# Chunked scan of a hybrid decoder layer: B transposed as two row tiles, and the z transposes placed ahead of the first twelve gate products

## What is computed

```python
def step(state, inp):
    xc, ac, bc, cc = inp
    cs = jnp.cumsum(ac, axis=1)
    seg = cs[:, :, None] - cs[:, None, :]
    lmat = jnp.exp(jnp.where(causal, seg, -jnp.inf))
    cb = jnp.einsum("blgn,bsgn->blsg", cc, bc)
    y_diag = jnp.einsum("blsg,blsgj,bsgjp->blgjp", cb, lmat, xc)
    y_off = jnp.einsum("blgn,bgjpn,blgj->blgjp", cc, state, jnp.exp(cs))
    decay = jnp.exp(cs[:, -1:] - cs)
    new_state = (state * jnp.exp(cs[:, -1])[..., None, None]
                 + jnp.einsum("blgn,blgj,blgjp->bgjpn", bc, decay, xc))
    return new_state, y_diag + y_off
...
y = y + xs * d_skip
yg = y * silu(z)          # then a norm over each group, and norm_w
gates = sigmoid(merge)    # merge is the last part of the input projection
```

## Time and profile before

| | us |
|---|---|
| median of 3 runs | 2771.94 |
| lowest, highest | 2771.37, 2773.98 |
| the profiled execution | 2769.81 |
| its span | 2768.2 |
| PE busy in it | 2684.8 |
| DVE, POOL, ACT busy | 1531.2, 1487.4, 1175.7 |

### The profile page before, as it was taken

The page is one execution under the profiler, slowest core; times in us unless marked ns, Lnnn a source line. Parts: engine busy times, 40 slices in busy tenths (PEclk is TensorE's granted clock), DMA queues, the critical chain, the costliest instruction groups (busy, mean ns, idle before and its releaser), DMA issues. The chain is left out here.

```text
span 2768.2 us, 45651 instructions
## 1 busy us (share of the span) xinstructions
PE 2684.8 (97%) x17046; PEld 2203.3 (80%) x17046; DVE 1531.2 (55%) x2475; ACT 1175.7 (42%) x2207; POOL 1487.4 (54%) x1055
## 2 busy tenths in 40 slices
PE   6999999999999999999999899999899999999998
PEld 5888888888887788888888677777788877788787
DVE  6335322599452523786532565665788885843432
ACT  6232232233223532333232556566677854532332
POOL 7778767777786777777875455454000254232000
PEclk8999999999999999999999999999999999999999
DMA  3557433333224333332233555564777578954543
GB/s 127 141 172 212 141 107 122 97 114 110 62 76 154 135 124 98 114 108 84 76 94 113 185 187 182 163 197 163 205 218 198 149 234 266 310 170 152 190 137 113
DMA packets 469469, 415.30 MB, mean 150 GB/s; under 512 B 43328, under 2 KB 414272, under 8 KB 464192
## 3 DMA queue, kind: packets, MB, share of 16 engines
q1 hardware_dynamic: 467008, 404.81, 47.4%
q0 software_dynamic: 2304, 8.39, 0.8%
HBM read 282.60 MB, written 130.55 MB: 149 GB/s over the span
## 5 line engine op out<-in xcount | busy, mean ns | idle before, releaser
L547 PE MATMUL p_acc<-h_kept,w_hi 128*128 128x512 f32 x1216 | 476.0, 391 | 6.5 <-ACT work L603 3.1
L549 PE MATMUL p_acc<-h_kept,w_lo 128*128 128x512 f32 x1216 | 474.6, 390 | 0.0
L548 PE MATMUL p_acc<-h_kept,w_hi 128*128 128x512 f32 x1216 | 474.6, 390 | 0.0
L428 POOL TENSOR_TENSOR w_lo<-p_sums,w_hi 128x512 fp32r<-128x512 f32 x300 | 387.5, 1306 | 149.3 <-ACT w_hi L644 149.3
L644 ACT ACTIVATE w_hi<-p_sums 128x512 fp32r<-128x512 f32 x300 | 189.7, 633 | 505.3 <-PE p_acc L549 482.9
L272 DVE TENSOR_TENSOR p_stage<-p_acc,work 128x512 f32<-128x512 f32 x172 | 138.2, 806 | 275.3 <-PE p_acc L549 267.9
L547 PEld LDWEIGHTS p_acc<-h_kept,w_hi 128*128 128x128 f32 x1216 | 228.9, 188 | 56.4 <-ACT work L603 3.3
L549 PEld LDWEIGHTS p_acc<-h_kept,w_lo 128*128 128x128 f32 x1216 | 229.1, 188 | 47.7
L548 PEld LDWEIGHTS p_acc<-h_kept,w_hi 128*128 128x128 f32 x1216 | 229.0, 188 | 46.9
L547 PE MATMUL p_acc<-p_ops,w_hi 128*128 128x512 f32 x608 | 238.2, 392 | 5.7 <-DVE p_ops L743 5.7
L548 PE MATMUL p_acc<-p_ops,w_hi 128*128 128x512 f32 x608 | 237.5, 391 | 0.0
(11 more groups left out here) (335 smaller groups left out, 6069.9 us busy)
## 6 DMA issues: line engine op xcount, KB each, us to landing
raw<-w_in SPq DMA_DIRECT2D x100, 512.0 KB, 4.7
work<-s_gates SPq DMA_DIRECT2D x48, 512.0 KB, 7.1
p_rawb<-w_in SPq DMA_DIRECT2D x38, 512.0 KB, 3.7
keep<-w_in SPq DMA_DIRECT2D x38, 512.0 KB, 4.8
s_xbc<-p_stage SPq DMA_DIRECT2D x32, 512.0 KB, 2.6
work<-s_xbc SPq DMA_DIRECT2D x16, 1024.0 KB, 6.3
att_all<-s_att SPq DMA_DIRECT2D x24, 528.0 KB, 5.2
s_gates<-p_stage SPq DMA_DIRECT2D x24, 512.0 KB, 6.0
```

The costliest lines, as they stand in the source:

```text
L428: tt(w_lo[:, k], weight(u, k), w_hi[:, k], ALU.subtract).then_inc(w_made, 1)
L547: pe.matmul(bank, hi, ops[k][:, 0, c], start=c == 0, stop=False)
L548: pe.matmul(bank, hi, ops[k][:, 1, c], start=False, stop=False)
L549: last = pe.matmul(bank, lo, ops[k][:, 0, c], start=False, stop=c == 3)
```

## The change

B is transposed by the helper `transpose_by_rows`: eight 64-row instructions in place of four of 128 rows. The upper rows go into the first half of the first bank of `ps_m`, the lower ones into half of a new bank `ps_b`. ACT copies B out in two instructions of 128x256 in place of one of 128x512. The wait for `out_taken` before it becomes an instruction of its own (`wait_alone`). The z transposes, with their two waits, move ahead of `gates(0)`, so that `gates(0)` and `gates(1)` stand in a row.

```diff
+        ps_b = s.ps("s_psb", [P, BANK])
...
+        b_banks = [ap[:, :GROUPS * P // 2].rearrange("p (g q) -> p g q", q=P // 2) for ap in (ps_m, ps_b)]
...
-                        pe.wait_ge(out_taken, 2 * c + 1)
+                        wait_alone(pe, out_taken, 2 * c + 1, turn_released)
                         for g in range(GROUPS):
-                            last = pe.transpose(ps_m[:, g * P:(g + 1) * P], b_t[:, g], ident[:])
+                            last = transpose_by_rows(pe, [b_bank[:, g] for b_bank in b_banks], b_t[:, g], ident)
                         last.then_inc(b_transposed, 1)
                         pe.wait_ge(out_taken, 2 * c + 2)
                         for g in range(GROUPS):
                             last = pe.matmul(ps_m[:, BANK + g * P:BANK + (g + 1) * P], b_t[:, g], c_t[:, g],
                                              start=True, stop=True)
                         last.then_inc(cb_ready, 1)
-                        gates(0)
                         pe.wait_ge(z_loaded[k], 16 * i + 16)
                         wait_alone(pe, x_tok_ready, c + 1, turn_released)
                         for b in range(KC):
                             last = transpose_by_rows(pe, [z_bank[:, b] for z_bank in in_banks(ps_x)], z_t[:, k, b], ident)
                         last.then_inc(z_transposed, 1)
+                        gates(0)
                         gates(1)
...
-                        act.activation(b_tok[:], ps_m[:, :BANK], ACT.Copy).then_inc(b_tok_ready, 1)
+                        for half in range(2):
+                            at = slice(half * P // 2, (half + 1) * P // 2)
+                            last = act.activation(b_tok[:].rearrange("p (g q) -> p g q", q=P)[:, :, at], b_banks[half], ACT.Copy)
+                        last.then_inc(b_tok_ready, 1)
```

## The result

The changed kernel takes 2779.25 us (median of 7 runs, 2775.37 to 2780.55); the kernel before took 2769.41 us beside it (7 runs, 2764.96 to 2773.98). The ratio is 1.0035, with a 95% interval of 1.0023 to 1.0047: slower by about 9.8 us. Its profiled execution has a span of 2776.2 us, 8.0 us more than before.

The account below looks back on a forecast made before the run. PE, busy 97% with in-order work, was taken as the bound; 7.9 - 0.6 + 4.1 = +11.4 us on 2771.9 gave 2783.3 us, with 2781 to 2786 by the bounds (73%) and 2776 to 2789 as the 8-in-10 range.

Parts of the forecast that it names:

- the two signs of a wrong forecast: z starting before the copy of x ends behind a load, or granted clock leaving 1.00 between 1560 and 1958.
- The exposed wait: Chunks 2 to 12, even: PE waits 1.48 us before z for ACT's copy of x; net 6 x 1.31 = +7.9 us.
- Joined products and odd chunks: Odd chunks and chunk 14: joining blocks saves 0.17 us, z waits 0.1; nine times, -0.6 us, bounds -1.2 and 0.
- Chunk 0: Scan's first chunk: moved products no longer fit before z, +2.4 us, plus 1.7 for the clock; +4.1 us.
- The low clock: Chunk 0, behind z: after some 4 us of waiting products may run at half speed; +1.7 us, bounds 0 and 2.5.
- B as row tiles: B before CB: a shorter B only leaves PE waiting for ACT's second copy of y; 0 us.
- The second copy on ACT: ACT's copy of B in two: 0.1 to 0.2 us of mask delay, hidden by 0.6 us of cover; cost 0.
- The table load: ACT, before the copy of x in chunks 0, 2 to 12: 1.28 us, without the skill's drain of about 1.38 us.
- The faster one: Rival: no wait before z, shorter pieces gain 0.42 us in each of 16 chunks, 6.7 us, about 2765; 4%.
- The absorbed one: Rival: later PE waits and a quicker B absorb half the loss, some +5.7 us, 2777.5; 9%.
- The falling clock: Rival: clock drops to 0.50 in every even chunk, 1.5 to 1.7 us more in six, +10, about 2793; 9%.
- The 1.75 us gap: Merge stage: a gap longer than the new 1.5 us wait, followed by clock 1.00; cited against the falling clock.

Follow-up runs that it names:

- e12: The changed kernel, unchanged, measured and profiled again; ratio 1.0041 to the kernel before, scan stage 444.2 us.
- e2: Kernel before with only the z transposes moved ahead of gates(0), B as before; ratio 1.0042 to the kernel before.
- e4: Changed kernel with ACT's loop cut behind the odd chunk's square root, so no table load precedes the copy of x; ratio 1.0008 to the kernel before.
- e5: Changed kernel with ACT's copy of x cut into eight copies of 128x128; one run, scan stage 460.1 us against 443.0.
- e9: Kernel before with B as row tiles and y's second half copied out by DVE beside ACT; ratio 0.9988 to the kernel before.
- e7: Changed kernel with the first pair of chunks written out on PE and gates(0) ahead of z in chunk 0 only; ratio 1.0037 to the kernel before.
- e13: The kernel of e7, unchanged, measured and profiled again; ratio 1.0032 to the kernel before, scan stage 439.7 us.
- e8: Changed kernel with ACT's loop cut so no table load precedes the copy of x, and gates(0) ahead of z in chunk 0; ratio 1.0016.

## Why the prediction held

The forecast was 2783.3 us, +11.4 us, from 2776 to 2789. Measured were 2779.25 us and a ratio of 1.0035, 9.7 us. That lies in the range, but below the 2781 to 2786 us that the bounds of the working gave and that had 73% of the chances. Two things put it there. The base had moved: the kernel before had 2769.4 us over seven runs where three had given 2771.9. And the kernel lost 9.7 us, where the stage in which the working placed the loss lost 11.3. The 1.6 us between them are less than the scatter of other stages and of the runs: the same kernel again, e12, gave a ratio of 1.0041, 11.3 us.

That 11.3 us stand against 11.4 is partly luck: three terms were off, by -0.3, +0.6 and -0.3 us, and cancelled, and a second profile of the changed kernel had a stage 1.2 us longer. The mechanism is not luck. z did start 0.10 us after the end of ACT's copy, and the granted clock was 1.00 from 1560 to 1960 us, so neither of the two signs of a wrong forecast showed.

- **The exposed wait (+7.9).** Right in place, number and size. CB to z was foretold as 1.48 us behind CB's 0.91, that is 2.39 us, and was 2.38 or 2.39 in all six chunks; 6 x 1.26 = 7.6 us came of it. e2, e4 and e5 show the cause apart from everything else.
- **Joined products and odd chunks (-0.6).** The saving of 0.17 us a chunk is real, but z starts 1.09 us behind CB where the first product started at 0.91. In odd chunks the copy of x had ended 0.22 us before, so it is not what holds z. The forecast's reason was that CB is still draining; no run tests that. The 0.18 us are what was named as the upper bound; 0.1 was taken. So nothing is left: 0 in nine chunks, and 1.26 us instead of 1.31 in the even ones.
- **Chunk 0 (+4.1).** 3.8 us. z started as foretold at the copy's end. The low clock did come: z to group 0 took 7.74 us, where 6.34 were worked out at the full clock, 1.4 us for the 1.7 assumed. This size varies: in e12 z to group 0 took 8.19 us and in e2 8.96, so 1.9 and 2.6 us for the clock. The other 0.3 us are that z started 7.47 us behind x, where it had been 7.79 before. B's row tiles did not save them, as e12 has them too and took 7.75 us. What holds ACT there, ahead of the table load and the copy, is the DMA of `s_sums` (3.54 us of waiting before, 3.31 after), and its landing varies.
- **B as row tiles (0).** The value was right and its reason was not. I had CB held by ACT's second copy of y, 0.05 us before it. In e9 that copy came early and CB stayed where it was. The two times had only coincided: B itself, released by the first copy, sets CB. By the twofold speed of the Trainium skill (TensorEngine Tiling (Array Packing), "Theoretical Speedup") B would have shrunk from 0.49 to 0.25 us by the forecast's estimate. Here B to CB went to 0.39 us, and B's start, later by 0.09 us, took that back.
- **The second copy on ACT (0)** was covered: group 0 of odd chunks stands where it stood.
- **The table load.** The page ScalarE: Activation LUTs of the Trainium skill has a drain beside the load ("What ACT_TABLE_LOAD costs"). In chunk 4 after the change the load starts at 1646.04 and the copy at 1647.33: 1.29 us in all, with nothing added, and the wait that hangs on it had the size of the rows.
- **The rivals.** The faster one fell with the order of ACT: with the load moved (e4) even chunks did become like odd ones, as it said, but they gained nothing beyond that. The absorbed one did not happen in the stage. The falling clock did not happen in the changed kernel's even chunks, in two profiles, but four times behind the longer waits of e5. The 1.75 us gap taken as evidence against it is thus no safe bound, as e5's waits of 1.67 us are shorter.

## What to carry to other kernels

Before moving work that stands between a producer and the piece that waits for its consumer, write down what the other engine does in that time, with its table loads: here twelve products were the cover for 2.3 us of ACT. A table load that the compiler sets at the top of a loop body belongs to where the loop is cut, so that cutting the loop elsewhere moves it off the path without touching the order of work. A piece that ends just when its successor is released says nothing about which of the two sets the time; take one away before paying for the other. And where two engines' instructions hold each other up, look at which started first: one and the same pair cost PE a wait of 1.1 us in one chunk and nothing in the next.

## What the runs showed of the hardware

The granted clock fell to 0.50 although no single gap of PE was long. In e7's chunk 4 it fell at about 1642.8, amid the transposes and CB, behind a wait of 1.19 us and ahead of the z wait; the fall cost 2.1 us. In e5 it fell behind waits of 1.67 us in four chunks of six, for 1.6 us each, and stayed at 1.00 in two with the same wait. Behind the 29 waits of 1.2 us it never fell. The same kernel as e7, run again as e13, had no fall.

A DVE addition of 128x1024 took 1.22 to 1.23 us with no POOL split of 128x1024 beside it, and up to 3.43 us when the split had started first. It then ended 1.08 to 1.09 us after the split in 168 cases of 168, as if it had begun at about the split's end. Where the addition had started first, in e8's chunk 3, it took 1.23 us and the split 3.27 against 2.39.

One program's attention stage took 240.9 and 232.3 us in two profiles, a difference almost as large as the whole effect measured here. Eight ACT copies of 128x128 took 1.47 us against 1.02 for one of 128x1024, so a copy more costs 0.06 us there.
